# Two blocks and a gathered expert layer on one core: GpSimd keeps at most two gathers in flight

## The reference

```python
q = (h @ w_q).reshape(B, S, 8, 2, 128)
sc = einsum('bshpd,phnd->bshpn', q, keys)
v1, i1 = top_k(sc[..., 0, :], 16);  v2, i2 = top_k(sc[..., 1, :], 16)
cand = v1[..., :, None] + v2[..., None, :]        # 256 candidates a head
best, pos = top_k(cand, 16);  idx = ...           # rows of u and v, 0..16383
gates = softmax(best)
ue = take(u, idx);  act = gelu(einsum('tkd,td->tk', ue, h))
ve = take(v, idx);  out = einsum('tk,tkd->td', gates * act, ve)
x = rms_norm(x + out, norm_final_g)
```

## Time and profile before

| | us |
|---|---|
| median of 3 runs | 1728.86 |
| lowest and highest | 1720.82, 1728.88 |
| the profiled execution | 1726.55 |
| its span, from the first to the last instruction | 1725.3 |
| first gather issued | 975.04 |
| last gather issued | 1706.06 |

### The profile page before, as it was taken

How to read it: one execution, slowest core, us unless ns; L and a number is a source line. 1 busy time by engine, 2 the same in 40 slices (tenths; PEclk the granted TensorE clock), 3 DMA queues, 4 the chain that set the end, 5 groups by cost and what they waited for, 6 DMA issues and landing times.

```text
span 1725.3 us, 19276 instructions
## 1 busy us (share of the span) xinstructions
PE 1504.8 (87%) x7183; PEld 1083.1 (63%) x7183; DVE 1079.1 (63%) x1970; ACT 661.9 (38%) x1102; POOL 547.5 (32%) x608
## 2 busy tenths in 40 slices
PE   7999999999999999999999888988677666777676
PEld 6888897888788788888899764543232222222222
DVE  5766645686664676675656675647675566666544
ACT  5545534785453555453725231222221121212111
POOL 1000001211000000000100356666666666766664
PEclk9999999999999999999999999999889888998899
DMA  8556454333353455564344889999999999999997
GB/s 282 179 187 195 149 183 158 106 134 105 122 183 111 157 195 195 182 187 156 123 132 164 282 319 352 367 367 367 374 365 375 376 377 373 378 367 357 362 372 294
DMA packets 199943, 431.87 MB, mean 250 GB/s; under 512 B 20774, under 2 KB 114091, under 8 KB 199851
## 3 DMA queue, kind: packets, MB, share of 16 engines
q0 software_dynamic: 73728, 268.47, 40.7%
q1 hardware_dynamic: 123312, 159.66, 28.5%
q10 hardware_dynamic: 2810, 2.52, 0.5%
HBM read 429.55 MB, written 1.05 MB: 250 GB/s over the span
## 4 chain that ended last, share of the span: by engine, by line
PE 52%; DVE 12%; issue 10%; POOL 9%; ACT 7%; another core or an unknown queue 5%; DMA 3%; DVEq 2%; ACTq 0%; POOLq 0%
PE ps L431 51%; POOL GS L2696 5%; POOL RAW L2696 3%; DVE WL L1786 3%; ACT WH L1260 2%; DMA RAW<-in_peer_u_dram,AR 2%; DVE GS L2535 1%; POOL AR L2696 1%; ACT AR L1744 1%; DVE RAW L2535 1%; DMA GS<-in_peer_v_dram,AR 1%; DVE XN L1823 1%; DVE H L1828 0%; DVEq L2367 0%
## 5 line engine op out<-in xcount | busy, mean ns | idle before, releaser
L431 PE MATMUL ps<-XX,WH 128*128 128x256 f32 (+1 forms) x1872 | 467.5, 330 | 9.7 <-DVE XX L1842 5.1
L1786 DVE TENSOR_TENSOR WL<-RAW,WH 128x2048 fp32r<-128x2048 f32 x135 | 309.7, 2294 | 187.0 <-ACT WH L1260 186.4
L431 PE MATMUL ps<-XX,WL 128*128 128x256 f32 x1288 | 364.3, 283 | 0.0
L431 PE MATMUL ps<-GS,AR 128*128 128x512 f32 x526 | 270.5, 650 | 107.2 <-issue 48.7
L431 PEld LDWEIGHTS ps<-XX,WH 128*128 128x128 f32 x1872 | 316.7, 192 | 47.2 <-issue 7.4
L1260 ACT ACTIVATE WH<-RAW 128x2048 fp32r<-128x2048 f32 x129 | 247.1, 1915 | 95.3 <-PE ps L431 95.1
L431 PEld LDWEIGHTS ps<-GS,AR 128*128 128x128 f32 x526 | 103.1, 206 | 263.9 <-issue 203.6
L431 PEld LDWEIGHTS ps<-XX,WL 128*128 128x128 f32 x1288 | 246.8, 192 | 0.7
L2586 POOL TENSOR_TENSOR small<-small 128x1 f32<-128x1 f32 x28 | 15.4, 557 | 683.0 <-DVE small L1818 365.3
L431 PE MATMUL ps<-RAW,AR 128*128 128x512 f32 x348 | 174.1, 632 | 47.2 <-issue 32.4
L2535 DVE CUSTOM_DVE_ANT_0 GS<-GS,ps 128x1024 f32<-128x1024 f32 x135 | 163.0, 1217 | 59.1 <-DMA GS<-in_peer_u_dram,AR 47.1
(11 more groups left out here) (377 smaller groups left out, 1872.9 us busy)
## 6 DMA issues: line engine op xcount, KB each, us to landing
RAW<-in_ffn_w_gu_dram SPq DMA_DIRECT2D x44, 1024.0 KB, 5.1
RAW<-in_w_in_dram SPq DMA_DIRECT2D x39, 1024.0 KB, 5.2
RAW<-in_ffn_w_down_dram SPq DMA_DIRECT2D x22, 1024.0 KB, 5.0
RAW<-in_w_out_dram SPq DMA_DIRECT2D x12, 1024.0 KB, 5.0
RAW<-in_xa_wkv_dram SPq DMA_DIRECT2D x8, 1024.0 KB, 5.4
RAW<-in_xa_wq_dram SPq DMA_DIRECT2D x4, 1024.0 KB, 5.3
RAW<-in_xa_wo_dram SPq DMA_DIRECT2D x4, 1024.0 KB, 5.1
RAW<-in_w_peer_q_dram SPq DMA_DIRECT2D x4, 1024.0 KB, 5.3
```

Of the source, the lines that this page charges most:

```text
L431: return nc.tensor.matmul(out_, lhsT, rhs, start=start, stop=stop, skip_group_check=True)
L1786: nc.vector.tensor_tensor(conv(1, k, kt), v, conv(0, k, kt).bitcast(F32), ALU.subtract).then_inc(S["lo"], 1)
```

## The change

GpSimd keeps a list `flying` of the last two gathers that it has issued. Before it issues another, and before its waits for the slot and for the list of rows, it waits until the older of the two has landed in full: the semaphore of that gather's slot at the value `v`. Two gathers can so be under way when an instruction of GpSimd ends, never three. The order of the gathers, their slots and all else stay.

```diff
+        flying = collections.deque()
         for what, n in SCHEDULE:
...
                     m = row // 16
-                    s, _ = slot[name, row]
+                    s, v = slot[name, row]
                     who, k = slot_free[name, row]
+                    if len(flying) == 2:
+                        pool.wait_ge(*flying.popleft())
+                    flying.append((S["gather%d" % s], v))
                     if who in pe.named:
```

## The result

| | us |
|---|---|
| changed kernel, median of 4 runs (lowest, highest) | 2322.44 (2314.01, 2325.76) |
| kernel before in the same measurement, median of 4 | 1725.16 |
| ratio, 95% interval | 1.347 (1.344 to 1.350) |
| predicted | 2154 (2050 to 2290) |

The change makes the kernel 35% slower. The prediction had the direction and what sets the new pace, but 25%, and the measured time lies 32 us above its range.

A forecast was written before the change was run, and what follows sets the result against it. Gathers near the DMA bandwidth limit, five in flight, would become latency-bound: two per 4.32 landing plus 0.24 waking, 4.56 us. 975.04 + 255 x 4.56, last issue 2140.1, plus 12.3 and 1.25: 2154 us (2050 to 2290), 25% slower.

The forecast's parts named there:

- the gather after the pause: U gather issued at 1317.12 in the kernel before, after GpSimd paused 3.85 us; its dot came 4.32 us later.
- rival (c): Gather stage: a lone gather lands within 2.62 us, so two feed the DMA engines; no slowdown or a gain, 1627 us; chance 0.02.
- (d): Added waits do nothing, each landing named being an older one of the same slot; 1728 us; chance 0.01.
- (e): Gather stage: slot pauses stay on top of the landing waits; at most 2237 us; chance 0.06.
- The landing: Gather stage: from a gather's issue to its use with no more than one other under way, 4.32 us.
- the first kind: Landings of gathers issued just after a GpSimd pause, 4.32 and 4.31 us, against 5.42 for the third after one.
- rival (a): Gather stage: the landing stays long at 5.42 us, a step of 2.83, 2435 us; chance 0.08.
- Rival (b): Gather stage: with more room behind it the landing shortens to 3.07 us, step 1.66, 1834 us; chance 0.06.
- Waking GpSimd: Delay of GpSimd's issue after a landing, beyond the delay already in the 4.32 us: 0.24 us, bounds 0 to 0.30.
- What the longer step hides: Gather stage: VectorE's 449 us and TensorE's 556 us fit under the longer step, and 83.3 us of slot waits go.
- the list of unit 1: List of rows awaited at gather 24; its work comes some 7 us later, covered by that gather being 13 us later.
- The end: From the last gather's issue to the span's end: landing 4.32, one addition 0.75, then 7.2; 12.3 us against 19.2 before.

The follow-up runs named there:

- e1_one: The changed kernel with one gather in flight in place of two, each issue waiting for the last one's landing; 3306.82 us.
- e7_half_one: The changed kernel with one gather in flight in place of two and rows of 2 KB in place of 4 KB; 2841.68 us.

## Why the prediction was right and wrong

**What bounds the kernel, and that two are too few: right.** Five in flight, 6.46 us from issue to use, a step of 1.25: the change turned a stage near the limit of bandwidth into one of latency. The 4.32 us of the gather after the pause said so, and rival (c), in which two in flight would have fed the DMA engines, was as unlikely as I had it. The waits do what they say (d), and no slot pauses came on top (e).

**The landing: wrong, 4.32 us where 5.0 was measured.** The step that failed is the sentence "With two in flight and 2.3 us between issues, the one before is well advanced when the next begins, so I take the first kind, 4.32." By the forecast's own numbers it was not advanced enough: a landing of 4.32 less a step of 2.28 leaves 2.04 us of the one ahead, just above the edge at 2.0. On it a late landing makes the next one late as well, and the kernel settles at 5.0 and a step of 2.6, which leaves 2.4. The trace of before had the other kind too, 5.42 us for a gather with others close ahead. I had it as rival (a), with a chance of 0.08, and the truth lies a little past half way from the forecast to it. The choice between two ends 1.1 us apart was made without asking what set the first kind apart. It was not that the one ahead was well advanced, for it had 1.8 to 1.9 us left there as well; it was that its packets were through before those of the next began, 1.65 us after the issue.

**The range: too narrow on that side.** Its upper end took a landing of 4.87, half way to (a), for an extreme. The landing is multiplied by 255. With an unknown between 4.32 and 5.42 and no row read in between, the range had to reach to (a) itself, 2435 us.

**Rival (b), a shorter landing: out.** The landing of a gather that meets no other is 4.2 us (e1_one), not the 3.07 of the rival, and the room behind it shortened nothing. The Trainium skill, DMA: Bandwidth & Descriptors, "Anatomy of one DMA", has a fit by which it would be an estimate of 3.2 us. The trace disagrees with that by 1.0 us.

**Waking GpSimd: right.** 0.24 us after VectorE in the rows of the changed kernel, as it was after ScalarE in the earlier trace rows.

**What the longer step hides: right.** TensorE's matmuls got slower, as this row shows beside the earlier trace rows, at a granted clock of 0.78 on average in place of 0.92:

```profile
L431 PE MATMUL ps<-GS,AR 128*128 128x512 f32 x521 | 378.5, 867 | 295.4 <-DMA GS<-in_peer_v_dram,AR 282.4 <-ACT AR L1744 13.0
```

Four times 0.87 are 3.5 us in two steps of 5.23, so this stayed under cover, but with a smaller margin than the 2.6 in 4.56 that I had reckoned with. VectorE and the list of unit 1 were covered, as forecast. **The end: right**, 12.9 us for 12.3.

**The signs to look for.** Idle times that end with landings, a DMA share near 0.6 (0.67) and hardly a wait for TensorE came; the rate is 201 GB/s in place of 230. I had named a step above 2.6 as the sign of (a). It came out at 2.617, on that mark and below the 2.83 of (a).

## What to carry to other kernels

A limit on the transfers in flight sets a stage's pace to (landing + wake-up) / limit as long as that is well above the pace of the issues themselves; with four here it gave 1.50 us where 1.56 was measured. The landing in that sum has to be read where as many are in flight as the limit allows, at the spacing that follows; neither a lone one nor a full queue will do. If the trace has only those two, both go into the range. And "the one ahead is nearly done" is a number to work out: what is left of it at the issue, against the time until the next one's packets start, here 2.0 us with the 0.34 behind the last packet. Before a limit is put in, compare landing / pace of the kernel as it runs, here 6.46 / 1.25: below five it binds, and from five on the wait does nothing good.

## What the runs showed of the hardware

A gather of 128 rows takes 4.2 us at 4 KB a row and 3.3 at 2 KB, issue to landing, with nothing else about (e1_one, e7_half_one): halving a row takes 0.9 us off, which leaves some 2.4 if the other half goes at the same rate. With the bytes the number of packets was halved too (40960 in the queue in place of 73728, each data packet still 4096 bytes), so the runs don't tell one from the other. By the fit of the Trainium skill, DMA: Bandwidth & Descriptors, "Anatomy of one DMA", the two would be estimates of 0.6 and 2.0. Of the 4.2 us, 1.65 pass before the first packet, some 2.3 are packets and 0.34 follow the last. With more than some 2.0 us left of the one ahead at its issue a gather takes 5.0 us, with three in flight 5.3, with four 5.7.

The DMA engines' busy share understates the room left. These are the windows of one and of four in flight, from the first issue to the last:

```profile
975.00:3292.90 2317.90, 980.11 (x1368) 351.95 (x1366) 464.53 (x1079) 149.03 (x396) 487.06 (x512) 0.61 0.39 116
```

```profile
975.00:1771.00 796.00, 559.99 (x1362) 234.27 (x1360) 460.26 (x1076) 147.96 (x396) 489.27 (x511) 0.97 0.94 337
```

116 GB/s at a share of 0.39, 337 at 0.94, and 201 at 0.67 with two. Per share that is 297, 359 and 300 GB/s, and 382 in the kernel before. With one or two in flight the same bytes hold the engines longer than with four or more, so at a share of 0.67 the rate could not be raised by a half but, as the kernel before shows, by four fifths.

TensorE's granted clock is 0.61 in the one and 0.97 in the other, with the same matmuls in both, and 0.78 with two in flight: from four to two to one in flight the same work, with longer stretches of standing still, was done at a lower clock. Without a limit, in the shortest stage, it is 0.92 and not above 0.97, so the length of the stage does not settle it alone. It was not what the kernel waited for.
